# Delta rule's loop: from slot 12 VectorE adds values and scaled reads ahead of one solve product, and key reads run a slot further ahead

## The reference

```
t_inv = inverse of (eye + strict lower part of (beta k k^T * decay))
u = t_inv @ (v * beta)
w = t_inv @ (k * beta * exp(gcum))
v_new = u - w @ s
o = (q * exp(gcum)) @ s + (q k^T * decay) @ v_new      (latent chunks only)
s = g_last * s + (k * exp(gcum_last - gcum))^T @ v_new
```

## Time and profile before

| | us |
|---|---|
| median of 3 runs | 2122.23 |
| lowest, highest | 2119.7, 2125.66 |
| profiled execution, its span | 2123.98, 2122.2 |
| PE busy | 2037.0 (96%) |
| DVE busy | 724.1 (34%) |
| ACT busy | 572.6 (27%) |
| slots 0 to 31 of the loop, first to last solve | 1573.20 to 1788.29 |

### The profile page before, as it was taken

One profiled execution on the slowest core, in us unless ns is written; L12 is line 12 of the kernel. 1 busy time (PEld: TensorE's weight loads), 2 busy tenths in 40 slices (PEclk: granted clock), 3 DMA queues, 4 the chain that ended last, 5 costly groups with the idle time before them and its releaser, 6 DMA issues.

```text
span 2122.2 us, 29477 instructions
## 1 busy us (share of the span) xinstructions
PE 2037.0 (96%) x12476; PEld 1252.9 (59%) x12476; DVE 724.1 (34%) x1441; ACT 572.6 (27%) x1224; POOL 88.4 (4%) x86
## 2 busy tenths in 40 slices
PE   7999999999998999999999999998989997999997
PEld 2444777776664444444444465444766665888886
DVE  2541676204672010000000046456757755010001
ACT  4211113524452020000000032224355788120000
POOL 0000231000000000000000000000111110000000
PEclk9999999999999999999999999999989999999999
DMA  6343100133301212212222122112224210234442
GB/s 270 122 181 122 40 32 29 63 136 120 121 2 40 89 60 80 79 65 75 79 74 69 60 100 99 60 60 80 82 81 169 73 55 9 99 139 146 152 149 90
DMA packets 28001, 193.53 MB, mean 91 GB/s; under 512 B 3004, under 2 KB 4285, under 8 KB 5854
## 3 DMA queue, kind: packets, MB, share of 16 engines
q1 hardware_dynamic: 27826, 191.51, 24.6%
q10 hardware_dynamic: 44, 0.14, 0.0%
HBM read 190.59 MB, written 1.05 MB: 90 GB/s over the span
## 4 chain that ended last, share of the span: by engine, by line
PE 87%; DVE 6%; ACT 4%; DMA 1%; issue 1%; SPq 0%; POOL 0%; DVEq 0%; ACTq 0%; POOLq 0%
PE psum L700 86%; ACT ws_sb L1474 1%; DVE ws_sb L1945 1%; DVE gl_tmp_sb L1945 1%; ACT arena_sb L1474 1%; DMA ring_sb<-w 1%; DVE hT_sb L1948 1%; DVE arena_sb L1945 1%; DMA xT_sb<-x 1%; DVE ws_sb L1948 0%; DVE arena_sb L1954 0%; PE psum L1089 0%; ACT const_sb L1474 0%; ACT wide_sb L1474 0%; ACT hT_sb L1474 0%
## 5 line engine op out<-in xcount | busy, mean ns | idle before, releaser
L700 PE MATMUL psum<-hT_sb,ring_sb 128*128 128x512 f32 (+2 forms) x2272 | 802.3, 514 | 5.8 <-ACT hT_sb L1474 3.3
L700 PEld LDWEIGHTS psum<-hT_sb,ring_sb 128*128 128x128 f32 (+1 forms) x2272 | 430.0, 190 | 369.5 <-issue 341.6
L700 PE MATMUL psum<-arena_sb,ring_sb 128*128 128x512 f32 (+1 forms) x1216 | 397.5, 489 | 5.0 <-DVE small_sb L1951 1.9
L1474 ACT ACTIVATE ws_sb<-psum 128x512 f32<-128x512 f32 (+3 forms) x256 | 141.2, 552 | 774.1 <-PE psum L700 743.8
L700 PEld LDWEIGHTS psum<-arena_sb,ring_sb 128*128 128x128 f32 x1216 | 232.7, 192 | 167.1 <-issue 143.8
L700 PE MATMUL psum<-ring_sb,hT_sb 128*128 128x256 f32 (+3 forms) x1248 | 245.6, 375 | 0.5 <-ACT hT_sb L1474 0.5
L700 PEld LDWEIGHTS psum<-ring_sb,hT_sb 128*128 128x128 f32 (+1 forms) x1248 | 196.0, 178 | 59.7 <-issue 28.3
L1945 DVE TENSOR_TENSOR arena_sb<-ws_sb,psum 128x512 f32<-128x512 f32 (+1 forms) x44 | 24.4, 554 | 414.7 <-PE psum L700 414.7
L1948 DVE SCALAR_TENSOR_TENSOR xT_sb<-psum,mod_sb,xT_sb 128x256 f32<-128x256 f32 x48 | 23.2, 483 | 388.1 <-PE psum L700 387.5
L1474 ACT ACTIVATE wide_sb<-xT_sb 128x512 f32<-128x512 f32 (+1 forms) x40 | 21.8, 544 | 400.5 <-PE psum L700 296.9
L1948 DVE SCALAR_TENSOR_TENSOR ws_sb<-ws_sb,cols_sb 128x512 f32<-128x512 f32 (+1 forms) x176 | 123.7, 703 | 6.3
(11 more groups left out here) (165 smaller groups left out, 1468.1 us busy)
## 6 DMA issues: line engine op xcount, KB each, us to landing
ring_sb<-w SPq DMA_DIRECT2D x154, 1024.0 KB, 4.8
hT_sb<-w SPq DMA_DIRECT2D x16, 1024.0 KB, 4.8
ring_sb<-w SPq DMA_DIRECT2D x8, 768.0 KB, 4.1
xT_sb<-x SPq DMA_DIRECT2D x1, 2048.0 KB, 12.6
const_sb<-consts SPq DMA_DIRECT2D x1, 2048.0 KB, 9.5
y<-xT_sb SPq DMA_DIRECT2D x1, 1024.0 KB, 4.8
ring_sb<-w SPq DMA_DIRECT2D x2, 256.0 KB, 3.7
const_sb<-consts SPq DMA_DIRECT2D x1, 512.0 KB, 5.6
```

The lines of the kernel that those rows point to most:

```text
L700: return nc.tensor.matmul(o, l, r, start=start, stop=stop)
L1474: return nc.scalar.activation(o, i, func, **kw)
```

## The change

The values and the scaled reads are added ahead of the product, from slot 12 on, by VectorE: `add_values(i)` computes `v1 - exp(gcum) * BR` for four heads in four multiply-adds into `g_r`, which now has two buffers. `solve(i)` then issues only the 8 products with this sum. ScalarE scales reads only for slots 4 to 11, ahead of `take`, no longer behind it. `reads` move one slot ahead: slot i issues reads i+2. On VectorE `add_values(i+1)` stands first in slots 11 to 30, and outputs are collected a slot later in the order, ahead of the update. `scale_state` waits for its slot's key reads itself.

```diff
-        g_r = area(ws, 8192, 4, P)
+        g_r = (area(ws, 8192, 4, P), area(extra, 2560, 4, P))
+        SUMMED = 12
@@ TensorE, solve
-                    if c > 0:
+                    if i >= SUMMED:
+                        pe.wait_ge(G["v_added"], i - SUMMED + 1)
+                    elif c > 0:
                         pe.wait_ge(G["r"], i - 3)
...
+                            if i >= SUMMED:
+                                last = mm(o, y, g_r[i % 2][rows, v, :])
+                                continue
                             last = mm(o, y, v1[rows, j, (4 * g + v) * P:(4 * g + v + 1) * P], stop=(c == 0))
                             if c > 0:
-                                last = mm(o, y, g_r[rows, v, :], start=False)
+                                last = mm(o, y, g_r[i % 2][rows, v, :], start=False)
@@ TensorE, reads
                     pe.wait_ge(G["s"], i - 3)
-                    if i > 4:
+                    if i > SUMMED:
+                        pe.wait_ge(G["v_added"], i - SUMMED)
+                    elif i > 4:
                         pe.wait_ge(G["r"], i - 4)
@@ TensorE, loop
-                    if 3 <= i < 31:
-                        reads(i + 1)
+                    if 2 <= i < 30:
+                        reads(i + 2)
@@ ScalarE, read_scaled, scale_state, loop
-                    act.wait_ge(G["x"], i)
+                    act.wait_ge(G["x"], i - 1)
...
+                    act.wait_ge(G["ks"], i - 3)
...
+                    if 3 <= i < SUMMED - 1:
+                        read_scaled(i + 1)
                     take(i)
-                    if 3 <= i < 31:
-                        read_scaled(i + 1)
@@ VectorE
+                def add_values(i):
+                    dve.wait_ge(G["ks"], i - 3)
+                    dve.wait_ge(G["x"], i - 1)
+                    for v in range(4):
+                        at = (4 * g + v) * P
+                        ins = stt(g_r[i % 2][:, v], psum[:, BR, v * P:(v + 1) * P], neg_eg[:, e, 4 * g + v:4 * g + v + 1],
+                                  v1[:, j, at:at + P], ALU.mult, ALU.add)
+                    own(ins.then_inc(G["v_added"], 1), G["v_added"])
@@ VectorE, loop
+                    if SUMMED - 1 <= i < 31:
+                        add_values(i + 1)
                     if i >= 24:
                         collect_reads(i)
...
+                    if i > 16:
+                        collect(i - 1)
                     if i < 28:
                         update(i)
...
-                    if i >= 16:
-                        collect(i)
...
+                collect(31)
```

More of the change, by code:

```diff
@@ L603, in backbone @@
             dec seg exp kk mul mask r_init r_out z z_copied off inv diag
-            ks r x vs_taken vn_taken sd s s_scaled q q_scaled q_taken o o_taken
+            ks r v_added x vs_taken vn_taken sd s s_scaled q q_scaled q_taken o o_taken
             """.split()}
@@ L1824, in read_scaled @@
                     act.wait_ge(G["ks"], i - 3)
-                    act.wait_ge(G["x"], i)
+                    act.wait_ge(G["x"], i - 1)
                     for v in range(4):
-                        ins = f(g_r[:, v], psum[:, BR, v * P:(v + 1) * P], ACT.Copy, scale=neg_eg[:, e, 4 * g + v:4 * g + v + 1])
+                        ins = f(g_r[i % 2][:, v], psum[:, BR, v * P:(v + 1) * P], ACT.Copy, scale=neg_eg[:, e, 4 * g + v:4 * g + v + 1])
                     own(ins.then_inc(G["r"], 1), G["r"])
@@ L2298, in update @@
                     own(ins.then_inc(G["s"], 1), G["s"])
+                def add_values(i):
+                    c, g = i // 4, i % 4
+                    ty, ab, j, e = chunk(c)
+                    dve.wait_ge(G["ks"], i - 3)
[5 more added lines that the diff above has]
+                    own(ins.then_inc(G["v_added"], 1), G["v_added"])
                 def merge(i, heads):
```

## The result

| | before | changed |
|---|---|---|
| median of 20 runs, us | 2122.57 | 2129.2 |
| lowest, highest | 2116.46, 2128.09 | 2122.39, 2135.1 |
| ratio | 1 | 1.0026, 95% interval 1.0017 to 1.0036 |
| profiled execution, its span | 2123.98, 2122.2 | 2122.39, 2120.6 |

The changed kernel is slower: by the ratio 0.26%, 5.5 us, by the two medians 6.6 us (0.31%), which lies in the interval too. The interval does not hold 1, so it is slower indeed, by about the 0.3% that I called a difference that can be told. The profiled execution is the fastest of its 20 and says nothing by its span: its first solve starts at 1568.18, that of before at 1573.20, after identical code (over all traces of this study it starts between 1568.2 and 1577.4).

What follows compares the result with a forecast made beforehand. TensorE's order of work was taken as the bound. +0.7 +1.2 +7.3 -6.0 -5.3 +3.0 = +0.9 on 2122.23 gave 2123 us, with 2112 to 2135 for 8 in 10.

Steps and rivals of the forecast that it cites:

- slots 2 to 10, reads a slot earlier: Slots before 11: reads moved to slots 2 to 29 save nothing there; 0.7 us late at slot 11.
- hole in slot 11: Slot 11: reads wait for addition 12 behind update 10, 4.23 us against 3.02 on TensorE; 1.2 us lost.
- state step 11 to 20, without the clock: Slots 11 to 20, from state step to state step: 73.2 us against 65.9, so 7.3 us lost.
- clock: Slots 11 to 20: holes bring two or three falls to 1.2 GHz, some 1.6 us each; +3.0 us.
- state step 20 to 27: Slots 21 to 27: 40.2 us against 46.25, so 6.0 us gained.
- state step 27 to first mixing: Slots 28 to 31 and on to the mixing of heads: no loop through VectorE, 5.3 us gained.
- The new wait: Reads two slots ahead wait for VectorE's addition behind the last update: 4.23 us from state step to reads.
- the signs named: Expected traces: state step 11 to 20 73 us; slots 11 to 19 TensorE under 60 us busy; plain slots 5.2.
- Rival (a): Half clock through the slots with holes, 11 to 20: +11 to +16 for +3, 2131 to 2137 us; chance 0.20.
- Rival (b): TensorE stays the bound, as VectorE adds early enough that no reads wait: 2101 us; chance 0.05.
- (c): Half the gain: VectorE's pieces run closer than added, or the tail gives 3 us more: about 2114 us; chance 0.13.
- rival (d): Elimination and loop cost more than summed, additions at 1.3 us, slots 14 to 19 3 us more: 2129 to 2131; chance 0.10.

Runs made afterwards that it cites:

- fill: The changed kernel with 56 idle products added in the holes of slots 12, 13, 15 and 16: 1.0005 of the kernel before.
- m12: The changed kernel with the addition for slot i+2 directly ahead of update i, instead of i+1 at the slot's start: 0.9951 of the kernel before.
- mm20: m12 with additions and single products from slot 20 and ScalarE's scaling of reads two slots ahead: 0.9926 and 0.9928 of the kernel before.

## Why the prediction was right where it was, and the terms that were not

The forecast was 2123, no change, range 2112 to 2135; measured 2129.2, slower by about the bound. That is inside the range and outside the 2117 to 2128 that I had called the forecast itself. Step by step, from the profiled executions:

| term | worked out | trace |
|---|---|---|
| slots 2 to 10, reads a slot earlier | +0.7 | +0.7 (slot 2 to slot 11: 66.64 for 65.92) |
| hole in slot 11 | +1.2 | 1.20 |
| state step 11 to 20, without the clock | +7.3 | +13.3 with the clock: 79.25 for 65.92 |
| clock | +3.0 | in the line above, with slot 20's 0.8: 6.1 |
| state step 20 to 27 | -6.0 | -5.7 (40.58 for 46.25) |
| state step 27 to first mixing | -5.3 | -5.4 (27.97 for 33.39) |

The new wait is the one named, with 4.3 to 4.5 us from state step to reads in slots 12 and 13, and the holes came at 1.20, 2.32, 2.12, 1.71, 2.84, none, 2.27, 0.61, 0.73, 1.61 for the 1.2, 2.3, 2.1, 2.3, 2.9, 2.6, 2.4, 1.6, 0.7, 1.6 worked out. Where one is short or missing (slots 14, 16 and 18), the clock was low before it; in the second trace of the changed kernel slots 14 and 18 have 2.32 and 1.60. Slot by slot, from solve to solve, the 65.4 us worked out for slots 12 to 19 (1.01 for the query reads of slot 15 included) hold wherever a trace of the changed kernel or of fill ran at 1.00: 8.60 for 8.55 in slot 12, then 6.46 for 6.41, 8.01 for 7.98, 8.33 for 8.33, 9.13 for 9.10, 8.33 for 8.32 and 7.46 for 7.40 in slots 14 to 19; slot 13, at 0.92, took 9.39 for 9.33. Plain slots took 5.29 for 5.24, slot 28 4.29 for 4.3, slot 29 3.77 for 4.0, slot 30 4.71 for 4.5. TensorE's 17.7 us of saved products were so turned into waits and low clock: m12 shows it by getting 14 us back without a product more or less. Of the signs named, two did not come: state step 11 to 20 took 79 us, not 73, and TensorE was busy 65.8 and 62.8 us in slots 11 to 19, not under 60. Both are the clock's.

What was off is, first, a size in the step called **Clock**: "I expect two or three falls of this size", +3.0. Their number was right, three in the first trace and two in the second, but not their size: 10.2, 6.8 and 3.4 us at 1.2 GHz, 10.2 and 3.4 in the second, where the fall of before lasted 3.4. Slots 12 to 19 took 70.7 and 69.5 us for the 65.4 worked out without the clock, so it cost 5.2 and 4.1 us for +3.0. Second, slot 20 in the +7.3: 8.76 was worked out, 9.60 and 9.88 measured at 1.00, as its off-diagonal half has the "issue" hole shown above and took 2.9 and 3.2 us for 2.14. What that hole waits for is open. Third, the baseline: the trace of before had a fall that cost 1.5 us in slot 15 and that its second trace had not, and I took its length as typical.

By traces this adds up. The first pair differs by 4.1 us, 3.2 more than the +0.9: 2.2 by the clock, 0.8 by slot 20. The second pair differs by 5.3 us, 4.4 more: 1.1 by the clock, 1.1 by slot 20, 1.5 by the baseline, 0.4 by slots 0 and 1, which this change leaves as they were, and 0.3 by slots 21 to 27. One trace each is no better than some 2 us, so the shares in the 5.5 to 6.6 us of the 20 runs are not divided further. The small total of the forecast rests on terms of 7 and 11 us against each other; each was confirmed by itself within 1 us, the clock apart, so it was not luck.

Rival (a), the half clock through all slots with holes, did not come in full: granted clock over slots 11 to 19 is 0.87 and 0.91, not under 0.7, and the time lies between the forecast and its 2131: its mechanism was there at a quarter to a half of its price. Rival (b) is refuted by the holes, (c) by the tail, which gave what was summed. The time lies in the 2129 to 2131 of rival (d), but not for its reason: additions took 1.12 to 1.13 us for four as in the earlier trace rows, and slots 14 to 19 at 1.00 took what was summed.

The Trainium skill (TensorE: Matmul & The Clock Gate, Part 1: The HAM clock gate) puts the fall down to an idle array and calls its moment variable. That it varies is borne out: the first fall of the changed kernel was in slot 13 in one trace and in slot 12 in the other. That the array has to stand idle for it is not borne out by the profile's busy time: mm20 fell in a stretch with no hole, as the last section shows.

## What to carry to other kernels

When work is moved from a bound engine to one with idle time, ask what the new instruction stands behind in that engine's order: 12 us of idle time in front of a wait are worth nothing to work that is queued behind the wait. Draw the cycle state, update, addition, reads, state and add up its latency; if it exceeds the bound engine's slot, put the new work ahead of the waiting instruction, here one call moved and 14 us. Ahead of the waiting instruction the new work can still make that engine's queue the bound, as in slots 15 to 17 of m12. Reading ahead needs its consumer moved ahead as well, or it waits for the consumer's old place.

## What the runs showed of the hardware that was not expected

TensorE's clock fell to 1.2 GHz with the engine busy throughout by the profile (whose ends of products are modelled). Windows of mm20's first trace, slots 12 and 13, and its timeline at the fall:
```profile
1658.14:1665.28 7.14, 7.14 (x187) 5.16 (x185) 5.91 (x12) 4.87 (x15) 1.68 (x3) 1.00 0.44 149
1665.28:1674.79 9.51, 9.51 (x194) 6.62 (x193) 4.01 (x13) 8.27 (x17) 1.04 (x1) 0.84 0.32 115
```
```profile
1661.10 2.21 PE L701 MATMUL psum<-ring_sb 32*32 32x32 f32 x128
1663.24 1.04 PE L701 MATMUL psum<-hT_sb,small_sb 128*2 128x512 f32 x8
...
1670.38 1.05 PE L701 MATMUL psum<-const_sb,extra_sb 128*128 128x2 f32 x8
1671.36 1.49 PE L701 MATMUL psum<-hT_sb,small_sb 128*2 128x512 f32 x8
1672.78 2.08 PE L701 MATMUL psum<-const_sb,arena_sb 64*128 64x256 f32 x8
```
The last hole of over 0.1 us before the fall ends at 1626.50, 45 us earlier. Among what ran before it in slots 12 and 13 are 256 products of 32x32 tiles, products that move 2 columns, and products that load 2. The clock falls at about 1671.8, within the row of 1671.36, and is back at about 1675.2; slots 13 and 14 took 1.6 us more than in the second trace of the same kernel, which stayed at 1.00. Over the 14 traces of the study the clock fell in slots 12 to 14 in six and in slots 15 to 16 in nine, in slot 17 and in slot 20 in one each; of these places slot 15 too has 2-column products. Whether the kind of product or something else decides was not separated by any run.
